# Last block's mix: two products per weight tile instead of three, with the halves added at the eviction

## What is computed

```python
h = rmsnorm_2(x, norm_w[l])
proj = h @ w_in[l]
# ... o_a, o_b, o_c: the three branches, from other columns of proj
branches = jnp.stack([o_a, o_b, o_c], axis=2)
branch_out = jnp.einsum('bsnc,ncd->bsnd', branches,
                        w_out[l].reshape(N_BRANCH, BRANCH_WIDTH, D_MODEL))
gates = jax.nn.sigmoid(gate_logits.reshape(bsz, s, N_BRANCH, D_MODEL))   # gate_logits: last columns of proj
x = x + jnp.sum(gates * branch_out, axis=2)
return rmsnorm_2(x, final_norm_w)
```

## Time and profile before

| | |
|---|---|
| median of 3 runs | 3758.92 us (3751.8 to 3780.71) |
| the profiled execution | 3780.5 us, span 3778.8 us |
| mean granted clock of TensorE in it | 0.973 |
| busy shares of the span | PE 95%, DVE 61%, ACT 49%, POOL 7% |

### The profile page before, as it was taken

The page is one execution under the profiler, slowest core; times in us unless marked ns, Lnnn a source line. Parts: engine busy times, 40 slices in busy tenths (PEclk is TensorE's granted clock), DMA queues, the critical chain, the costliest instruction groups (busy, mean ns, idle before and its releaser), DMA issues.

```text
span 3778.8 us, 76247 instructions
## 1 busy us (share of the span) xinstructions
PE 3574.6 (95%) x29380; PEld 3482.6 (92%) x29380; DVE 2288.7 (61%) x3280; ACT 1844.1 (49%) x2606; POOL 258.3 (7%) x328
## 2 busy tenths in 40 slices
PE   6989899999999998889988999999998999989998
PEld 5989899999999997788888999999997999989998
DVE  4987666556655534555555666566657648655554
ACT  3755455444444534344444555444444455574443
POOL 1762100000001000000002000000010000000000
PEclk9999999999999999998999999999998999999999
DMA  4555566566656543111124666766564655647664
GB/s 132 168 150 157 142 177 177 173 187 178 177 165 176 151 129 89 51 51 46 51 62 130 181 183 178 202 182 182 171 183 118 164 154 141 162 125 193 186 189 134
DMA packets 1103454, 561.76 MB, mean 149 GB/s; under 512 B 23011, under 2 KB 1101429, under 8 KB 1102981
## 3 DMA queue, kind: packets, MB, share of 16 engines
q1 hardware_dynamic: 1100672, 553.98, 52.3%
q10 hardware_dynamic: 1957, 2.83, 0.2%
q0 software_dynamic: 624, 2.13, 0.2%
HBM read 556.77 MB, written 2.10 MB: 148 GB/s over the span
## 4 chain that ended last, share of the span: by engine, by line
issue 90%; POOLq 6%; PE 2%; DVE 1%; ACTq 0%; ACT 0%; POOL 0%; DMA 0%; DVEq 0%
POOLq L820 4%; POOLq L481 1%; PE ps L495 1%; ACTq L2334 0%; DVE arena L526 0%; PE ps L436 0%; PE ps L438 0%; PE ps L437 0%; PE ps L2358 0%; POOLq L2501 0%; DVE ps L522 0%; POOLq L2504 0%; POOLq L2428 0%; DVE x_lo L520 0%; POOLq L484 0%
## 5 line engine op out<-in xcount | busy, mean ns | idle before, releaser
L320 DVE TENSOR_TENSOR w_lo<-raw,w_hi 128x1024 fp32r<-128x1024 f32 (+1 forms) x1136 | 1351.2, 1200 | 857.9 <-ACT w_hi L314 852.2
L314 ACT ACTIVATE w_hi<-raw 128x1024 fp32r<-128x1024 f32 (+1 forms) x1136 | 1143.1, 1015 | 606.9 <-PE ps L354 341.7
L352 PE MATMUL ps<-x_hi,w_hi 128*128 128x272 f32 (+1 forms) x2816 | 805.3, 286 | 17.8 <-DVE x_lo L520 17.8
L436 PE MATMUL ps<-x_hi,w_hi 128*128 128x256 f32 (+1 forms) x2640 | 757.6, 287 | 58.1 <-DVE w_lo L320 25.4
L353 PE MATMUL ps<-x_lo,w_hi 128*128 128x272 f32 (+1 forms) x2816 | 804.6, 286 | 0.0
L354 PE MATMUL ps<-x_hi,w_lo 128*128 128x272 f32 (+1 forms) x2816 | 804.5, 286 | 0.0
L437 PE MATMUL ps<-x_lo,w_hi 128*128 128x256 f32 (+1 forms) x2640 | 749.3, 284 | 0.0
L438 PE MATMUL ps<-x_hi,w_lo 128*128 128x256 f32 (+1 forms) x2640 | 749.0, 284 | 0.0
L436 PEld LDWEIGHTS ps<-x_hi,w_hi 128*128 128x128 f32 x2640 | 502.0, 190 | 67.5 <-DVE w_lo L320 27.9
L352 PEld LDWEIGHTS ps<-x_hi,w_hi 128*128 128x128 f32 x2816 | 535.5, 190 | 19.6 <-issue 19.5
L353 PEld LDWEIGHTS ps<-x_lo,w_hi 128*128 128x128 f32 x2816 | 535.6, 190 | 0.0
(11 more groups left out here) (497 smaller groups left out, 4882.7 us busy)
## 6 DMA issues: line engine op xcount, KB each, us to landing
raw<-ffn_w_up SPq DMA_DIRECT2D x352, 512.0 KB, 4.6
raw<-w_in SPq DMA_DIRECT2D x232, 512.0 KB, 3.8
raw<-cd_w_in SPq DMA_DIRECT2D x100, 512.0 KB, 3.8
raw<-ffn_w_down SPq DMA_DIRECT2D x128, 384.0 KB, 3.4
raw<-ab_w_in SPq DMA_DIRECT2D x80, 512.0 KB, 4.3
raw<-ffn_w_down SPq DMA_DIRECT2D x128, 320.0 KB, 3.3
raw<-w_out SPq DMA_DIRECT2D x48, 512.0 KB, 4.0
raw<-ab_w_out SPq DMA_DIRECT2D x32, 512.0 KB, 4.0
```

Source lines behind the costliest of these rows:

```text
L314: nc.scalar.activation(w_hi[:, j % SLOTS, 0:kt], raw[:, j % RING, 0:kt], ACT.Copy).then_inc(rounded, 1)
L320: nc.vector.tensor_tensor(w_lo[:, j % SLOTS, 0:kt], raw[:, j % RING, 0:kt], w_hi[:, j % SLOTS, 0:kt].bitcast(F32), ALU.subtract).then_inc( ...
L352: nc.tensor.matmul(acc, w_hi[:, j % SLOTS, k, 0:w], mh, start=first, stop=False)
L436: nc.tensor.matmul(acc, w_hi[:, j % SLOTS, k, 0:w], mh, start=(k0 + k == 0), stop=False)
```

## The change

In the mix alone, the high and low half of the input become one moving operand of 512 columns with a step between them (`x2` holds both halves in one allocation; `CAT_BOTH[n]` spans both halves of a branch result, `CAT_FAR[n]` tiles apart). `wide_product` issues, per k, one product of the high weights with both (512 columns, the whole bank) and one of the low weights with the high half (256 columns, the first half of the bank); at a job's last k in the other order. The second half of the bank then holds low x high weights and has to be added at the eviction: ACT copies it to SBUF, DVE adds the first half to it. For the gate ACT takes the sigmoid after that, in place; for the branch DVE multiplies and adds as before. ACT waits for DVE's sum (`gate_in`), DVE for ACT's copy (`half_out`) and sigmoid (`gate_made`). The four gate buffers become two, and two buffers `branch_in` take the room.

```diff
--- before.py
+++ after.py
@@ -195,8 +195,8 @@
     work2, _ = place("work2", [P, 2 * DK * X_W], F32, x_off)
     xm_hi, _ = place("xm_hi", [P, DK, T], F32R, x_off)
     xm_lo, _ = place("xm_lo", [P, DK, T], F32R, x_off + 4 * DK * T)
-    x2_hi, _ = place("x2_hi", [P, DK, SEQ], F32R, x_off)
-    x2_lo, _ = place("x2_lo", [P, DK, SEQ], F32R, x_off + 4 * DK * SEQ)
+    x2, _ = place("x2", [P, 2 * DK, SEQ], F32R, x_off)
+    x2_hi, x2_lo = x2[:, 0:DK], x2[:, DK:]
     spare, _ = place("spare", [P, 2048], F32, x_off + 8 * DK * SEQ)
     lam_at, _ = place("lam_at", [P, 40])
     vec, _ = place("vec", [P, NROWS])
@@ -415,6 +415,16 @@
                 at[0] += 1
         return upto
 
+    def wide_product(j, k, bank_, both, hi_at, at_k, kt):
+
+        halves = ps[:, bank_].rearrange("p (a b) -> p a b", a=2)
+        hi_weight, lo_weight = w_hi[:, j % SLOTS, k], w_lo[:, j % SLOTS, k]
+        if at_k == kt - 1:
+            nc.tensor.matmul(halves[:, 0], lo_weight, both[:, hi_at], start=False, stop=False)
+            return nc.tensor.matmul(halves, hi_weight, both, start=False, stop=True)
+        nc.tensor.matmul(halves, hi_weight, both, start=(at_k == 0), stop=False)
+        return nc.tensor.matmul(halves[:, 0], lo_weight, both[:, hi_at], start=False, stop=False)
+
     def stream_tensor(pe, name, operand):
 
 
@@ -432,6 +442,12 @@
                         bank_free(pe, name, 0, u)
                     pe.wait_ge(split, p.base + v + RING + 1)
                 mh, ml = operand(u, k0 + k)
+                if isinstance(ml, int):
+                    last = wide_product(p.base + v, k, bank(name, u), mh, ml, k0 + k, kt)
+                    if k == n - 1:
+                        last.then_inc(multiplied, 1)
+                    at[:] = [v, k + 1] if k < n - 1 else [v + 1, 0]
+                    continue
                 acc, j = ps[0:w, bank(name, u), 0:mh.shape[-1]], p.base + v
                 nc.tensor.matmul(acc, w_hi[:, j % SLOTS, k, 0:w], mh, start=(k0 + k == 0), stop=False)
                 nc.tensor.matmul(acc, w_hi[:, j % SLOTS, k, 0:w], ml, start=False, stop=False)
@@ -1796,11 +1812,16 @@
     LRU_T = order("gates0", "gates1")
 
 
-    CAT_HI = {n: nc.alloc_sbuf_tensor_at(f"cat_hi{n}", [P, CW, S2], F32R, offset=arena_off + 4 * SLOT * at_) for n, at_ in ((2, 2), (0, 0), (1, 9))}
-    CAT_LO = {n: nc.alloc_sbuf_tensor_at(f"cat_lo{n}", [P, CW, S2], F32R, offset=at_) for n, at_ in
-              ((2, arena_off + 4 * SLOT * 6), (0, arena_off + 4 * SLOT * 8), (1, x_off + 8 * DK * SEQ))}
+    CAT_FAR = {2: 4 * CW, 0: 8 * CW, 1: (arena_off + 4 * SLOT * 9 - x_off - 8 * DK * SEQ) // (4 * S2)}
+    CAT_BOTH = {n: nc.alloc_sbuf_tensor_at(f"cat{n}", [P, CAT_FAR[n] + CW, S2], F32R, offset=at_) for n, at_ in
+                ((2, arena_off + 4 * SLOT * 2), (0, arena_off), (1, x_off + 8 * DK * SEQ))}
+    CAT_NEAR, CAT_END = ({n: CAT_BOTH[n][:, first:first + CW] for n, first in at_} for at_ in
+                         (((2, 0), (0, 0), (1, 0)), CAT_FAR.items()))
+    CAT_HI = {2: CAT_NEAR[2], 0: CAT_NEAR[0], 1: CAT_END[1]}
+    CAT_LO = {2: CAT_END[2], 0: CAT_END[0], 1: CAT_NEAR[1]}
     CAT = {2: slot(6), 0: slot(8), 1: slot(10)}
-    gate = view(arena, 7 * SLOT, 4, S2)
+    gate, branch_in = view(arena, 7 * SLOT, 2, S2), view(arena, 7 * SLOT + 512, 2, S2)
+    half_out, gate_in, gate_made = sem("half_out"), sem("gate_in"), sem("gate_made")
     cat_hi_made, cat_lo_made, summed = sem("cat_hi_made"), sem("cat_lo_made"), sem("summed")
 
     def cat_high(act, n):
@@ -1815,18 +1836,37 @@
     def gate_scalar(act, u, g):
 
         result_ready(act, ph["two"], 0, u)
-        if g >= 4:
-            act.wait_ge(summed, g - 3)
-        nc.scalar.activation(gate[:, g % 4], ps[:, bank("two", u), 0:S2], ACT.Sigmoid).then_inc(drained[bank("two", u)], 1)
+        if g >= 2:
+            act.wait_ge(summed, g - 1)
+        nc.scalar.activation(gate[:, g % 2], ps[:, bank("two", u), S2:], ACT.Copy).then_inc(half_out, 1)
+        act.wait_ge(gate_in, g + 1)
+        nc.scalar.activation(gate[:, g % 2], gate[:, g % 2], ACT.Sigmoid).then_inc(gate_made, 1)
+
+    def branch_scalar(act, u, g):
+
+        result_ready(act, ph["two"], 0, u)
+        if g >= 2:
+            act.wait_ge(summed, g - 1)
+        nc.scalar.activation(branch_in[:, g % 2], ps[:, bank("two", u), S2:], ACT.Copy).then_inc(half_out, 1)
+
+    def gate_vector(dve, u, g):
+
+        dve.wait_ge(half_out, 2 * g + 1)
+        nc.vector.tensor_tensor(gate[:, g % 2], ps[:, bank("two", u), 0:S2], gate[:, g % 2], ALU.add).then_inc(drained[bank("two", u)], 1)
+        dve.drain().then_inc(gate_in, 1)
 
     def branch_vector(dve, u, g):
 
         x = h[:, MIX[g][1], META:]
-        result_ready(dve, ph["two"], 0, u)
-        result_out(dve, "two", 0, u - 1)
-        nc.vector.tensor_tensor(gate[:, g % 4], ps[:, bank("two", u), 0:S2], gate[:, g % 4], ALU.mult).then_inc(drained[bank("two", u)], 1)
+        dve.wait_ge(half_out, 2 * g + 2)
+        nc.vector.tensor_tensor(branch_in[:, g % 2], ps[:, bank("two", u), 0:S2], branch_in[:, g % 2], ALU.add).then_inc(drained[bank("two", u)], 1)
         dve.drain()
-        nc.vector.tensor_tensor(x, x, gate[:, g % 4], ALU.add).then_inc(summed, 1)
+        dve.wait_ge(gate_made, g + 1)
+        nc.vector.tensor_tensor(gate[:, g % 2], branch_in[:, g % 2], gate[:, g % 2], ALU.mult)
+        dve.drain()
+        nc.vector.tensor_tensor(x, x, gate[:, g % 2], ALU.add).then_inc(summed, 1)
+
+    WIDE = ('mix',)
 
     def two_scalar(act):
         keep = {"cz": c_z, "f": h_b, "q": h_q, "i": h_v, "az": h_z, "bz": l_z}
@@ -1842,7 +1882,9 @@
                 g = t // 2
                 if t % 2 == 0:
                     gate_scalar(act, u, g)
-                elif MIX[g][0] == BRANCHES[-1]:
+                else:
+                    branch_scalar(act, u, g)
+                if t % 2 and MIX[g][0] == BRANCHES[-1]:
                     act.wait_ge(summed, g + 1)
                     square_tile(act, "out", 0, MIX[g][1], 2, META)
                 return
@@ -1995,6 +2037,8 @@
                 mm.then_inc(drained[bank("two", u)], 1)
             elif name == "mix" and t % 2:
                 branch_vector(dve, u, t // 2)
+            elif name == "mix":
+                gate_vector(dve, u, t // 2)
         upto = stream(dve, "two", split_part, work)
 
 
@@ -2188,9 +2232,11 @@
                 n = MIX[t // 2][0]
                 if k == 0 and t < 6 * MIXED:
                     pe.wait_ge(cat_lo_made, 2 * BRANCHES.index(n) + 2)
-                return CAT_HI[n][:, k], CAT_LO[n][:, k]
+                return CAT_BOTH[n][:, k:k + CAT_FAR[n] + 1:CAT_FAR[n]], int(n == 1)
             if u == 0 and k % 4 == 0:
                 pe.wait_ge(norm_lo[5], k // 4 + 1)
+            if name in WIDE:
+                return x2[:, k:k + DK + 1:DK], 0
             return x2_hi[:, k, 0:S2], x2_lo[:, k, 0:S2]
         upto = stream_tensor(pe, "two", operand)
```

## The result

| | before | changed |
|---|---|---|
| median of 20 runs each | 3766.2 us (3746.3 to 3792.7) | 3787.3 us (3772.5 to 3806.9) |
| ratio of changed to before | | 1.0054, 95% interval 1.0035 to 1.0073 |
| the profiled execution's span | 3778.8 us | 3794.1 us |

The changed kernel is slower by some 20 us, 13 to 27 by the interval. That is within 1%, as forecast, but it is clear of noise, it has the other sign than the forecast, and the median lies outside the range given. The kernel before has 3766.2 by 20 runs, where the prediction started from 3758.9 by three.

A forecast was written before the change was run, and what follows sets the result against it. PE's product pace was taken to bound the long stretch, ACT's order of work the LRU stretch. 17.5 us saved less 9.2 and 0.9 lost gave 7.4 less: 3758.9 to 3751.5, say 3752 us; range 3731 to 3782.

The forecast's parts named there:

- The wide product: Mix, 512-column product on PE: claimed 218 ns, with the narrow one 335.7 ns a k, 17.4 less than before.
- The upper bound: Mix, highest time allowed for the 512-column product: twice the narrow one, 235.4 ns, a k of 353, no gain.
- rival (b): Mix products: one product less saves nearly nothing, so LRU stretch and end decide, +10 us, 3769 us; chance 0.28.
- The term of 17.5 us: Mix, last 126 parts of 8 k: 1008 k at 17.4 ns saved each, 17.5 us less.
- the second pace: 256-column products on PE: the same form goes at 113.0 and 117.7 ns, so an old k can cost 339.
- The LRU stretch: Start of the mix, LRU work woven between first gates: new eviction delays ACT and DVE, PE 9.2 us late.
- walk: Start of the mix: step-by-step reckoning of ACT, DVE and PE through the first gates, ending PE 9.2 us late.
- the four forecast: Start of the mix: four PE waits for the gate's bank, released by DVE's new sum, restarts at about 3369 and 3388.
- The steady exchange: Long stretch of the mix: the new ACT and DVE work at eviction fits in spare time and costs nothing.
- Rival (c): Pairs that square: ACT-DVE exchange overruns, PE waits 1 us in each of 30 pairs, 3799 us; chance 0.07.
- The end: Behind the last product, before the final norm: added copy and sum from the bank, +0.9 us.
- The sum: Whole kernel: 17.5 us less from products, 9.2 and 0.9 us added, net 7.4 us less.

The follow-up runs named there:

- e2_cut: Changed kernel with the 512-column product cut into two of 256 except at each job's first and last k, new eviction kept; 3771.4 us, ratio 1.0021.
- e13_two_again: Second profile of e10_two's kernel: 340 ns a k in gates 6 and 7, 353.1 from gate 8 on.
- e9_one: Kernel before plus one unused fp32 product of 128 columns ahead of gate 8 of the mix; 3772.9 us, ratio 1.0008.
- e10_two: Kernel before plus two unused fp32 products of 128 columns ahead of gate 8 of the mix; 3786.3 us, ratio 1.0033.
- e3_old_eviction: Changed kernel's wide products with the old eviction and four gate buffers, low input x high weights not added; 3779.1 us, ratio 1.0037.
- e5_columns: Kernel before plus unused product groups of 128 to 512 columns and three-product k groups between mix and final norm; those k groups took 5.42 to 5.62 us.
- e1_pace: Kernel before plus unused groups of products of several widths and layouts between mix and final norm; 512 columns took 234.2 ns, in one run or two.

## Why the prediction was wrong, step by step

**The wide product.** This is the step that failed first. The prediction took 218 ns for it, midway between an excess hidden in a long product and the row of 272 columns. It takes 234, and the narrow one 118.5 for the 117.7 taken. The reading "11.1 ns of each product are not columns" was right as arithmetic and wrong as a price per product: what the wide product pays grows with its columns. The upper bound, twice the narrow product (235.4), was the true value, and rival (b) had its mechanism. The rows held a hint: 272 columns cost 10.0 ns more than 256 at 113.0 did, for 16 columns, where the clock allows 6.7. The term of 17.5 us was 0.4 in the profile (353.3 against 352.9 over 1008 k). Why a column of this form costs more than the clock's time is not shown.

**What a row at one pace is worth.** The prediction took the profiled 353 ns a k as what the change works on, while it named the second pace and treated it as noise for both kernels alike. It is not alike: three products of 256 go at 340 in most profiles, one of 512 and one of 256 never did. Against ten profiles at 340 and three at 353.3 (mean 343.1) the wide form loses 9.8 ns a k, 9.9 us over 1008 k. e2_cut, e13_two_again and the time between e9_one and e10_two show that the pace is worth this much; its share of 10 in 13 is a count and not more.

**The LRU stretch** was right in its mechanism and in size: +9.2 forecast, +8.5 measured to gate 6 against the first profile, and e2_cut and e3_old_eviction put it on the eviction. That profile too is one of several: in the 13 with the old form gate 6 lies between 73.8 and 75.8 us, 74.96 as a mean, and against this mean the loss is 9.1. Moved back by the 5.9 us between the traces, the sigmoid of gate 0 ends at 3337.1 (walk 3337.0), the sum of gate 1 at 3352.6 (3352.7), PE restarts at 3368.6 and 3387.6 (3369.1 and 3388.35), at 3399.4 for gate 5 (3400.5) and at 3409.8 for gate 6 (3410.6). Each restart came 0.5 to 1.1 early. The walk added up durations, where operations behind each other start closer: a split's successor 1.14 us behind its start and not 1.23 (as rows 9 already show, 3389.77 to 3392.05 for two), a rounding's 0.96 and not 1.05. The wait of 0.64 us for gate 1's bank was missed: five waits for the four forecast.

**The steady exchange** cost nothing: no wait of PE between 3416 us and the last product. Rival (c) was wrong. **The end**: from the last product's start to the norm's first product 2.73 us before, 3.76 after, +1.0 for the 0.9 forecast.

**The sum.** 9.1 + 1.0 + 9.9 = 20.0 us, where the runs show 21 between the medians and 20.3 between the means. Rival (b) with its 10 us lacked the third term. Even with it, it would have said 3758.9 + 20 = 3779, inside the range; the measured 3787 lies outside because the median of three runs that all is counted from lay 7 us below that of twenty. "A median can move by 10 either way" was written down but not added to the upper end.

## What to carry to other kernels

Before joining products to save their fixed cost, measure the pace at two widths that lie apart: what a product takes beyond its columns at the clock may grow with the columns, and then joining gains nothing. A new step between two engines cost nothing here where both had spare time, and 9 us in six gates where their order of work set the pace, so walk the tightest stretch by rows. And where one form shows two paces in a trace, profile it several times and find out whether the changed form can have both, before one profile stands for the median.

## What the runs showed of the hardware that was not expected

- Long products of 4-byte (fp32r) operands at full granted clock take about 0.457 ns a column (384: 175.5 ns, 512: 234.2), with or without DMA and other engines at work, in one run or two. At granted clock 0.50, 256 columns take 213.5 ns, 0.83 a column, which is one column a cycle at 1.2 GHz. With 2-byte operands 256 and 512 columns take 109 and 216 ns.
- A product of 4-byte operands with its weight load took 111 to 112 ns at 128 columns and 113 at 192: fewer columns than 256 gained almost nothing.
- A stream of 256-column products has two steady paces, 113.3 and 117.7 ns. Behind an odd number of fp32 products of 128 columns it had the lower in the five groups of e5_columns, the eight of e1_pace and four profiles (which had it already), behind an even number the higher in three groups and three profiles. Behind the eight LRU products of gate 1 it had either, in one and the same program.
- The table load of ACT stood behind the operation ahead of the one that needs it: before the change in front of the wait for PE (3333.29 to 3334.57, the sigmoid at 3334.98), and behind the copy from the bank once that came between (3341.27 to 3342.55, the sigmoid at 3342.56), where its 1.28 us are no longer hidden.
